# A transformer step on one core: the later modulation moved from VectorE to GpSimd, the first modulation in four column tiles

## The chip, the cores and the metric

The kernel runs on one core of a Trainium2 chip. The core has five engines that run their own instruction streams and wait for each other by semaphores: TensorE (PE), VectorE (DVE), ScalarE (ACT), GpSimd (POOL) and SyncE (SP, here the queue that issues the transfers). The metric is the device time of one execution in microseconds. Before the change it is 2648.65 us, the median of 3 runs (2647.0 to 2650.12).

## The reference

One inference step of one layer for two request groups, a prompt of 2048 tokens and a sample of 64 tokens, with 1024 channels. Cut to what matters here:

```python
def adaln(c, w, b):
    m = jax.nn.silu(c) @ w + b
    return jnp.split(m, 3, axis=-1)          # shift, scale, gate: 1024 columns each

shift, scale, gate = adaln(c, mod_mix_w[l], mod_mix_b[l])   # "modulation" of the mixers
h = modulate(x, norm_mix_g[l], shift, scale)
q, k, v, rx, rg, ga, gb = jnp.split(h @ w_in[l], SPLIT_POINTS, axis=-1)
# mixer A: banded attention over q, k, v;  mixer B: conv4 + gated linear recurrence over rx, GeLU gate rg
merged = sigmoid(ga) * (attn @ w_branch[l, :512]) + sigmoid(gb) * (rnn @ w_branch[l, 512:])
x = x + gate * (merged @ w_out[l])
shift, scale, gate = adaln(c, mod_ffn_w[l], mod_ffn_b[l])   # modulation of the feed-forward part
h = modulate(x, norm_ffn_g[l], shift, scale)
val, gt = jnp.split(causal_dwconv(h @ ffn_up_w[l], ...), 2, axis=-1)
x = x + gate * ((val * gelu(gt)) @ ffn_down_w[l])
```

A modulation is a product of two rows (`silu(c)` of prompt and sample, 1024 long) with a 1024 x 3072 matrix. Shift and scale of the mixers are needed at once (the "first modulation", 2048 columns). The mixers' gate and all three parts of the feed-forward part (4096 columns, the "later modulation") are needed only after the attention.

## The kernel before

**Stages.** First modulation on TensorE (0 to 41 us of the profiled span); normalised and modulated input and the value product (to 143); 16 projection rounds (143 to 784); attention (to about 1030); merge, output product, feed-forward up (to 2213) and down. Large products use a seven-product scheme (Strassen's, with the parts of each operand split in two f16 terms, three passes each).

**A projection round** `r` (0 to 15) makes two column blocks of the input product in 21 products (7 combinations `c` times 3 column thirds `q`), each 12 matmuls of 128 x 352. Round `r` is of kind `r % 4`: 0 recurrence input, 1 and 3 gates, 2 and 3 q and k. In each round ACT copies products out of PSUM (`copy`, `c21`) and makes the high halves of the next round's weights (`proj_hi`), DVE adds blocks (`p_block`), makes weight sums (`proj_sums`) and low halves (`proj_lo`). The recurrence of mixer B is threaded through rounds `4j` to `4j+2` in six chunks `s`: `tap` (ACT), `conv` (3 dependent DVE instructions), `chunk_hi` (ACT), `chunk_lo` (DVE), `gate_products` (6 matmuls, PE line 3085, at fixed places between the 21 products), `gates` (ACT), `recur1`, `recur2`, `rnn_product`, `rnn_lo` (DVE), `root`, `rnn_hi` (ACT). PE runs in program order, so it stands when the gate products of a chunk wait for that chunk's `chunk_lo` (line 2299), or when a bank has not been read yet. In ACT's order the last half of a gate row (`gate_rows_v`, line 1463, which waits for DVE's last block of the round) stands ahead of `c21` (line 1450), and `c21` frees the banks of the next round's first product.

**The later modulation ("ring").** It is computed as rows: `silu(c)` is broadcast to all partitions (`crow`, 2 x 1024), and 32 weight tiles (128 x 1024) come in 64 half tiles of 128 x 512 (and 4 half rows of `c` before them) through two buffers `dmw`. `ring_load(k)` on SP waits until step `k - 2` has been used (semaphore `dm_used`), `ring_step(k)` on DVE multiplies and sums a half tile twice (lines 2362 and 2364), once for the prompt and once for the sample. The table `RING_AT` sets in which rounds, and at which of seven places in a round, how many steps stand: 12 in round 3, 14 each in 7 and 11, 6 each in 4, 8 and 12, 10 in 15. `gate_columns` in the merge stage reads the sums.

**What sets the order.** Every engine's order is written out by hand. SP's queue is in order as well: in each round it issues the next round's weights (`round_tiles`), the recurrent gate weights (`gw`), the stores of finished gate rows (`gate_row`), recurrent outputs (`recurrent_store`) and q and k rows (`head_row`), then the ring's loads of that round. After round 15 come the loads of the first attention group (`queries_and_keys`, line 827 and 830; `values_and_bias`, line 836 for the bias band), which may start when products 1 and 2 of round 15 are done. DVE's `mask(0)` (line 2467) needs the band. DVE's `p_block` of a round of kind 2 needs the gate rows of the round before stored (it writes over them).

**The first modulation.** `modulation(g)`, g in the order 0, 2, 1, 3, makes 512 columns: 8 float32 matmuls with the 2 columns of `silu(c)` as stationary operand, accumulated in PSUM partitions 0 and 1; `mod_row` (ACT) copies the row out, and 4 transposes of a 2 x 128 piece turn it to columns, of which DVE makes coefficients.

GpSimd does nothing in the rounds; it modulates half of the input at 42 to 127 us, scales probabilities in the attention, and makes weight and activation sums in the feed-forward part.

## Time and profile before

| | |
|---|---|
| time, median of 3 | 2648.65 us |
| profiled execution, time | 2646.2 us |
| its span | 2644.4 us |
| PE busy | 2577.5 us, 97% |
| DVE busy | 1777.0 us, 67% |
| ACT busy | 1357.8 us, 51% |
| POOL busy | 556.5 us, 21% |
| granted clock, mean | 0.995 |

The span is what the trace covers; the profiled execution's time is 1.8 us longer. Start times in the rows are microseconds from the span's start. An instruction's duration includes a tail in which the next may already run, so starts that follow each other are closer than durations (a DVE instruction of 0.53 us repeats every 0.44 to 0.45 us). The mean duration of a matmul is longer than its place in the stream for the same reason: 72 matmuls of a round take 10.9 us. Matmul records can be missing.

### The profile page before, as it was taken

The numbers are of one execution on the slowest core, as the hardware profiler recorded it, in microseconds if no ns is written. First come the engines' busy times: TensorE is split into PE (matmuls) and PEld (weight loads), VectorE is DVE, ScalarE is ACT, GpSimd is POOL, SyncE is SP. The second block draws the span as 40 slices with busy tenths as digits, with TensorE's granted clock in tenths as the row PEclk, the third lists the DMA queues.
The fourth block names the chain that finished last, engine by engine and source line by source line (L and its number), as shares of the span: only waits on it lengthen the run. The fifth ranks groups of instructions, "written<-read, shape, count | busy, mean of one in ns | idle before, by whom it ended". The sixth has DMA issues, their size and how long they took to land.

```text
span 2644.4 us, 49826 instructions
## 1 busy us (share of the span) xinstructions
PE 2577.5 (97%) x18148; PEld 1676.1 (63%) x18148; DVE 1777.0 (67%) x3411; ACT 1357.8 (51%) x2631; POOL 556.5 (21%) x645
## 2 busy tenths in 40 slices
PE   7999999999989999999999999999999999999998
PEld 2456666665656665559996666666666666666665
DVE  5967677666756665566777798888888874242433
ACT  4967374563747774124556556555655553121211
POOL 2600000000007773000000354334333321101000
PEclk9999999999999999999999999999999999999999
DMA  8621523334255542556552355545454439566662
GB/s 290 198 98 63 208 81 113 102 108 136 79 144 145 108 161 84 184 180 156 136 145 71 122 193 173 187 162 177 167 187 167 157 112 362 206 235 242 228 248 99
DMA packets 243602, 424.07 MB, mean 160 GB/s; under 512 B 58392, under 2 KB 163352, under 8 KB 235240
## 3 DMA queue, kind: packets, MB, share of 16 engines
q1 hardware_dynamic: 234584, 413.08, 47.2%
q10 hardware_dynamic: 8848, 8.74, 1.0%
q8 instruction: 104, 1.70, 0.3%
q14 instruction: 66, 0.54, 0.1%
HBM read 284.47 MB, written 139.92 MB: 160 GB/s over the span
## 4 chain that ended last, share of the span: by engine, by line
PE 67%; issue 3%; ACT 2%; DVE 2%; POOL 1%; DMA 0%; SPq 0%; DVEq 0%; ACTq 0%; POOLq 0%
PE ps L3044 38%; PE ps L3299 16%; PE ps L3153 6%; PE ps L3143 2%; PE ps L3125 2%; PE ps L3112 1%; ACT arena L1641 1%; DMA arena<-in_w_down 0%; ACT arena L1652 0%; POOL arena L1212 0%; ACT arena L1739 0%; DVE arena L2641 0%; DVE arena L2716 0%; DVE arena L2720 0%; PE ps L3190 0%
## 5 line engine op out<-in xcount | busy, mean ns | idle before, releaser
L3044 PE MATMUL ps<-arena 128*128 128x352 f16 (+1 forms) x11880 | 1614.2, 297 | 12.1 <-ACT arena L1450 8.1
L3044 PEld LDWEIGHTS ps<-arena 128*128 128x128 f16 x11880 | 1100.6, 97 | 520.9 <-issue 9.7
L3299 PE MATMUL ps<-arena 128*128 128x352 f16 x2772 | 414.8, 310 | 0.0
L3299 PEld LDWEIGHTS ps<-arena 128*128 128x128 f16 x2772 | 264.7, 96 | 150.2 <-issue 1.0
L1212 POOL TENSOR_TENSOR arena<-arena 128x640 f32<-128x640 f32 (+5 forms) x136 | 150.0, 1121 | 723.1 <-DVE arena L2496 721.7
L1231 POOL TENSOR_TENSOR arena<-arena 128x128 f32<-128x128 f32 x44 | 31.0, 705 | 748.8 <-DMA arena<-in_w_down 748.6
L3153 PE MATMUL ps<-arena 128*128 128x424 f16 (+1 forms) x960 | 171.5, 341 | 0.0
L1801 ACT ACTIVATE arena<-ps 128x352 f32<-128x352 f32 x264 | 116.3, 461 | 92.7 <-PE ps L3044 92.5
L2848 DVE TENSOR_TENSOR arena<-ps,arena 128x352 f32<-128x352 f32 x12 | 6.3, 525 | 206.9 <-PE ps L3299 176.7
L1432 ACT ACTIVATE arena<-ps 128x352 f32<-128x352 f32 x192 | 80.7, 464 | 122.1 <-PE ps L3044 121.9
L3153 PEld LDWEIGHTS ps<-arena 128*128 128x128 f16 x960 | 92.5, 96 | 78.6
L1241 POOL TENSOR_TENSOR arena<-arena 128x176 f32<-128x176 f32 (+1 forms) x57 | 53.0, 931 | 399.1 <-DMA arena<-ffn_hidden 399.0
L2648 DVE SCALAR_TENSOR_TENSOR arena<-arena 128x512 f16<-128x512 f32 x154 | 105.3, 716 | 44.1 <-ACT arena L1763 44.1
L2716 DVE SCALAR_TENSOR_TENSOR arena<-arena 128x2114 f32<-128x2114 f32 x44 | 109.9, 2498 | 27.0 <-ACT arena L1838 26.9
L1641 ACT ACTIVATE arena<-arena 128x640 f32<-128x640 f32 (+5 forms) x136 | 103.3, 760 | 45.9 <-DVE arena L2480 45.5
L1994 ACT ACTIVATE arena<-ps 128x352 f32<-128x352 f32 x12 | 5.6, 464 | 206.3 <-PE ps L3299 206.3
L1844 ACT ACTIVATE arena<-arena 128x1057 f32<-128x1057 f32 x44 | 45.4, 1078 | 125.5 <-DVE arena L2720 125.5
L2720 DVE SCALAR_TENSOR_TENSOR arena<-arena 128x2114 f32<-128x2114 f32 x44 | 109.0, 2476 | 0.3
L1838 ACT ACTIVATE arena<-arena 128x2114 f32<-128x2114 f32 x44 | 94.7, 2151 | 26.2 <-DVE arena L2703 25.7
L2480 DVE CUSTOM_DVE_ANT_0 arena<-ps,arena 128x640 f32<-128x640 f32 (+5 forms) x136 | 95.9, 737 | 10.5 <-issue 9.9
L3013 PE MATMUL ps<-arena 128*128 128x512 f16 (+1 forms) x408 | 91.6, 382 | 7.3 <-DVE arena L2130 5.4
L3125 PE MATMUL ps<-arena 128*128 128x128 f32 (+1 forms) x600 | 89.9, 282 | 4.7 <-POOL arena L1212 2.9
(237 smaller groups left out, 3303.0 us busy)
## 6 DMA issues: line engine op xcount, KB each, us to landing
hidden_combinations<-arena SPq DMA_DIRECT2D x48, 616.0 KB, 3.2
arena<-hidden_combinations SPq DMA_DIRECT2D x24, 1232.0 KB, 7.9
arena<-in_w_up SPq DMA_DIRECT2D x44, 512.0 KB, 5.1
down_combinations<-arena SPq DMA_DIRECT2D x44, 448.0 KB, 2.8
ffn_hidden<-arena SPq DMA_DIRECT2D x44, 440.0 KB, 3.1
arena<-down_combinations SPq DMA_DIRECT2D x10, 1792.0 KB, 7.7
arena<-down_combinations SPq DMA_DIRECT2D x20, 896.0 KB, 6.3
arena<-ffn_hidden SPq DMA_DIRECT2D x50, 352.0 KB, 3.9
```

The source lines that it names most:

```text
L1212: pool.tensor_tensor(own, own, inv[0:x.rows, x.tile % 2, x.h:x.h + 1].to_broadcast([x.rows, x.w]), ALU.mult).then_inc(p_scaled, 1)
L1641: act.activation(pr[b][0:x.rows, x.h, 0:x.w], pr[b][0:x.rows, x.h, 0:x.w], ACT.Exp, scale=-1.0, bias=least[0:x.rows, x.h:x.h + 1], accum_o ...
L1801: act.activation(fcp[(0, 1, 2, 0)[i]][q], ps[:, bank_of((0, 2, 3, 4)[i], q), 0:CF], ACT.Copy, scale=CSF)\
L1838: act.activation(out, u[:, 0:LF], ACT.Identity, scale=w0, bias=fb).then_inc(f_tap, 1)
L2480: dve.tensor_tensor_reduce(pr[x.tile % 2][0:rows, h, 0:w], src, bias[x.b][0:rows, h, x.b0:x.b0 + w], 1.0, 3.0e38, ALU.add, ALU.min, least[ ...
L2648: dve.scalar_tensor_tensor(fsp[:, c, :, 1, :], src.rearrange("p (k m) -> p k m", k=4), -WSF if c == 6 else WSF, fsp[:, c, :, 0, :], ALU.mu ...
L2716: dve.scalar_tensor_tensor(out, u[:, 1:1 + LF], tap(1), out, ALU.mult, ALU.add).then_inc(f_conv, 1)
L2720: dve.scalar_tensor_tensor(out, u[:, 2:2 + LF], tap(2), out, ALU.mult, ALU.add).then_inc(f_conv, 1)
L3044: mm = pe.matmul(out, wt[:, k, wp, :], act_t[:, k, hp], start=(first and k == 0 and n == 0), stop=(last and k == K - 1 and n == 2), skip_g ...
L3125: mm = pe.transpose(ps[0:k, bank, c0:c0 + x.rows], pr[x.tile % 2][0:x.rows, x.h, c * P:c * P + k], ident[0:x.rows, 0:x.rows])
L3153: mm = pe.matmul(out, wt[:, wp, k, :], mixT[:, k, hp, t:t + w], start=(k == k0 and m == 0), stop=(k == k1 - 1 and m == 2))
L3299: mm = pe.matmul(ps[:, down_bank(n, k), 0:CF].rearrange("p (w t) -> p w t", w=2), dwt(i)[:, wi, wp, :], dact[i][:, :, bi, hp, :], start=(i ...
```

## The change

The later modulation leaves DVE. The weight tiles are now taken by halves of the input columns: first columns 0 to 511 of `c` and of all 32 tiles (34 steps: 2 half rows of `c`, 32 half tiles), then columns 512 to 1023. `crow` is therefore only 2 x 512 and is loaded and put through tanh twice (rounds 0 and 8). DVE keeps four instructions (`ring_row`, two at the end of round 0 and two at the end of round 8). Each half tile is done on GpSimd in eleven instructions: two products of 128 x 512 and nine halving sums of both together (2 x 256, 2 x 128, ... 2 x 1), each waiting for the one before. SP's loads are spread by `RING_LOTS`: 5 in most rounds from 1 to 14, none in round 15, and in rounds of kind 1 and 2 they stand between the recurrent stores. ACT's wait for `dm_used` goes, as its scratch row is no longer used by the ring. The first modulation's 8 matmuls of a group use a stationary operand of 32 columns (2 filled, 30 zero), and matmul `k` writes PSUM partitions `32 * (k % 4)` onward; the four partial rows are added by the matmul that turns them to columns, whose moving operand `pick` has ones at the four places.

```diff
-        NRING = 4 + 64
-        RING_AT = {3: (2, 2, 2, 2, 2, 0, 2), 4: (2, 2, 2), 7: (2,) * 7, 8: (2, 2, 2), 11: (2,) * 7, 12: (2, 2, 2),
-                   15: (2, 2, 2, 2, 2)}
+        HALF_RING = 2 + 32
+        NRING = 2 * HALF_RING
+        RING_LOTS = (0, 5, 5, 5, 5, 5, 5, 4, 2, 6, 5, 5, 6, 5, 5, 0)
+        CROW_ROUND = 8
...
             def ring_load(k):
-                cols = slice(512 * (k % 2), 512 * (k % 2) + 512)
+                half, step = k // HALF_RING, k % HALF_RING
+                cols = slice(512 * half, 512 * half + 512)
+                if step == 0:
+                    keep_above_zero(sp, dm_used, k)
+                    for s in range(2):
+                        sp.dma_start(crowv[:, s, :], a["c"][s:s + 1, cols].to_broadcast([P, 512])).then_inc(crow_loaded, 16)
                 keep_above_zero(sp, dm_used, k - 1)
...
-                if i == 1:
-                    for s in range(3):
-                        recurrent_store(j, s)
-                if i == 2:
-                    for s in range(3, NS):
-                        recurrent_store(j, s)
+                if i in (1, 2):
+                    recurrent_store(j, 3 * i - 3)
+                    recurrent_store(j, 3 * i - 2)
+                    ring_loads(r, 0, 3)
+                    recurrent_store(j, 3 * i - 1)
+                    ring_loads(r, 3, RING_LOTS[r])
...
+            def ring_tile(half, n):
+                m, k = 32 * half + n, HALF_RING * half + 2 + n
+                w = dmw[k % 2]
+                pool.wait_ge(dmw_loaded[k % 2], 64 + 16 * (k // 2))
+                pool.wait_ge(dm_used, k)
+                keep_above_zero(pool, ring_folded, 9 * m)
+                pool.tensor_tensor(dprod[:, 0], w, crowv[:, 0, :], ALU.mult)
+                pool.tensor_tensor(dprod[:, 1], w, crowv[:, 1, :], ALU.mult).then_inc(dm_used, 1)
+                pool.wait_ge(dm_used, k + 1)
+                size = 256
+                for step in range(9):
+                    keep_above_zero(pool, ring_folded, 9 * m + step)
+                    out = dprod[:, :, 0:size] if size > 1 else dpart[:, 2 * n:2 * n + 2, half:half + 1]
+                    pool.tensor_tensor(out, dprod[:, :, 0:size], dprod[:, :, size:2 * size], ALU.add)\
+                        .then_inc(ring_folded, 1)
+                    size //= 2
...
-                if j and s == 0:
-                    act.wait_ge(dm_used, ring_before(4 * j + 1))
...
-                mm = pe.matmul(ps[0:2, 4 + g, :], csv[:, k, :], mw[:, 4 * g:4 * g + 4, k, :],
-                               start=(k == 0), stop=(k == KT - 1))
+                own = slice(32 * (k % 4), 32 * (k % 4) + 32)
+                mm = pe.matmul(ps[own, 4 + g, :], csw[:, k, :], mw[:, 4 * g:4 * g + 4, k, :],
+                               start=(k < 4), stop=(k >= 4), skip_group_check=True)
```

**DVE, second half of round 7, before.** L2267 is a `p_block` of sums, L2264 the last `p_block`, L2200 `proj_lo`, L2362 and L2364 the two passes of a ring step with their accumulator reads; the piece is the part from `proj_lo` 3 to the last `p_block`.

```order
L2200 SCALAR_TENSOR_TENSOR arena<-arena 128x4x128
L2362 ISA arena<-arena 128x512
L2362 ISA arena 128x1
L2364 ISA arena<-arena 128x512
L2364 ISA arena 128x1
L2362 ISA arena<-arena 128x512
L2362 ISA arena 128x1
L2364 ISA arena<-arena 128x512
L2364 ISA arena 128x1
L2264 SCALAR_TENSOR_TENSOR arena<-ps,arena 128x352 x2
L2264 SCALAR_TENSOR_TENSOR arena<-ps,arena 128x320
```

The same place in the changed kernel (L2234 is `proj_lo`, L2298 the last `p_block`, L2295 the first of round 8):

```order
L2301 TENSOR_TENSOR arena<-arena 128x320
L2301 TENSOR_TENSOR arena<-arena 128x32
L2234 SCALAR_TENSOR_TENSOR arena<-arena 128x4x128
L2298 SCALAR_TENSOR_TENSOR arena<-ps,arena 128x352 x2
L2298 SCALAR_TENSOR_TENSOR arena<-ps,arena 128x320
L2298 SCALAR_TENSOR_TENSOR arena<-ps,arena 128x32
L2234 SCALAR_TENSOR_TENSOR arena<-arena 128x4x128 x2
L2295 SCALAR_TENSOR_TENSOR arena<-ps,arena 128x352 x2
```

No ring pass stands between the weights' low half and the last block of the round.

**SP, from the q and k rows of round 15 to the bias band, before.** L758 to L764 store q, k and the new keys, L783 is the ring, L827 and L830 load queries and keys of the first attention group, L836 the band.

```order
L763 DMA out_k_prompt<-arena 128x512
L764 DMA out_k_sample<-arena 128x64
L758 DMA keys<-arena 256x1x2048
L759 DMA keys<-arena 256x1x64
L783 DMA arena<-in_w_mod_rest 128x512 x8
L827 DMA arena<-queries 64x2112 x2
L830 DMA arena<-keys 64x2x2048
```

In the changed kernel (L765, L766, L760 and L761 are the same stores, L836 and L839 the loads of queries and keys):

```order
L765 DMA out_k_prompt<-arena 128x512
L766 DMA out_k_sample<-arena 128x64
L760 DMA keys<-arena 256x1x2048
L761 DMA keys<-arena 256x1x64
L836 DMA arena<-queries 64x2112 x2
L839 DMA arena<-keys 64x2x2048
```

The ring's last eight loads no longer stand ahead of the attention's loads. In rounds 13 and 14 they now stand among the stores (L728 loads the round's weights, L772 stores recurrent outputs, L790 is the ring, L754 and L755 store gate rows):

```order
L772 DMA recurrent_outputs<-arena 256x1x353
L790 DMA arena<-in_w_mod_rest 128x512 x2
L728 DMA arena<-in_w_proj 128x1024 x2
L754 DMA gates<-arena 128x2048
L755 DMA gates<-arena 128x64
```

So the store of the gate rows, which a `p_block` of the next round waits for, is queued behind ring loads that GpSimd paces.

## Rows read from the trace of the kernel before

**Rows 1.** Waits of PE, 150 to 800 us: released by, us, times, longest

```profile
PE ps L3044 <- ACT arena L1450: 8.1, 5, 4.6
PE ps L3085 <- issue: 6.1, 4, 1.9
```

**Rows 2.** Timeline of PE in the rounds: start us, us, instructions, [idle before]

```profile
322.80 1.06 PE L3085 MATMUL ps<-arena 128*128 128x353 f16 x6 [1.94 <-issue]
462.34 21.64 PE L3044 MATMUL ps<-arena 128*128 128x352 f16 x144 [2.96 <-ACT arena L1450]
...
624.61 23.32 PE L3044 MATMUL ps<-arena 128*128 128x352 f16 x144 [4.61 <-ACT arena L1450]
```

**Rows 3.** Timeline of ACT at the end of round 11

```profile
622.06 1.91 ACT L1463 ACTIVATE arena<-arena 128x2048 f32<-128x2048 f32 x1 [10.48 <-DVE arena L2264]
```

**Rows 4.** Groups by form on DVE, 582.3 to 624.6 us (round 11)

```profile
L2362 DVE CUSTOM_DVE_ANT_0 arena<-arena 128x512 f32<-128x512 f32 x14 | 9.7, 691 | 7.5 <-issue 5.6 <-DMA arena<-in_w_mod_rest 1.1
```

**Rows 5.** Timelines at the rounds' end: SP, then DVE, then PE

```profile
754.98 16.29 SPq L783 DMA_DIRECT2D arena<-in_w_mod_rest  x8
...
779.19 0.45 SPq L836 DMA_DIRECT2D arena<-band  x1
...
791.86 0.17 DVE L2467 MEMSET arena<- 64x128 f32 x1 [12.66 <-DMA arena<-band]
...
790.48 0.59 PE L3112 MATMUL ps<-arena 128*128 128x128 f16 x4 [6.53 <-DMA arena<-keys]
```

**Rows 6.** Timelines at the start: ACT, then DVE

```profile
39.59 0.59 ACT L1361 ACTIVATE arena<-ps 2x512 f32<-2x512 f32 x1 [1.85 <-PE ps L2968]
...
40.68 0.50 DVE L2089 TENSOR_TENSOR arena<-ps,arena 128x4 f32<-128x4 f32 x4 [1.08 <-PE ps L2975]
```

**Rows 7.** Groups by form on POOL, whole span: busy us, mean ns

```profile
L1212 POOL TENSOR_TENSOR arena<-arena 128x512 f32<-128x512 f32 x8 | 8.2, 1040 | 3.2 <-DVE arena L2496 3.2
L1212 POOL TENSOR_TENSOR arena<-arena 128x128 f32<-128x128 f32 x8 | 3.2, 400 | 674.6 <-DVE arena L2496 674.6
```

**Rows 8.** Timeline of POOL, 1448 to 1450 us: the second waits for the first

```profile
1448.32 0.46 POOL L1231 TENSOR_TENSOR arena<-arena 128x128 f32<-128x128 f32 x1 [7.53 <-DMA arena<-in_w_down]
1448.86 0.45 POOL L1233 TENSOR_TENSOR arena<-arena 128x128 f32<-128x128 f32 x1
```

**Rows 9.** POOL and DVE at once: timelines, and line 2506 alone

```profile
1007.21 2.46 POOL L1212 TENSOR_TENSOR arena<-arena 128x640 f32<-128x640 f32 x2 [0.61 <-DVE arena L2496]
1008.45 2.30 DVE L2506 SCALAR_TENSOR_TENSOR arena<-arena 128x1024 f16<-128x1024 f32 x1
...
L2506 DVE SCALAR_TENSOR_TENSOR arena<-arena x8: 1216/1226/2297, 1008.5 to 1167.7; 128x1024 f16<-128x1024 f32 x8
```

**Rows 10.** Busy us by stretch: PE, PEld, DVE, ACT, POOL; rounds 5 and 6

```profile
342.80:383.10 40.30, 40.25 (x270) 26.12 (x271) 28.93 (x57) 32.11 (x54) 0.00 (x0) 1.00 0.12 41
383.10:421.60 38.50, 38.50 (x260) 24.90 (x258) 25.61 (x52) 24.48 (x46) 0.00 (x0) 1.00 0.29 99
```

**Rows 11.** Timelines of DVE and PE in rounds 5 and 6

```profile
357.56 0.52 DVE L2299 SCALAR_TENSOR_TENSOR arena<-arena 128x353 f16<-128x353 f32 x1
358.96 1.06 PE L3085 MATMUL ps<-arena 128*128 128x353 f16 x6
379.79 0.53 DVE L2299 SCALAR_TENSOR_TENSOR arena<-arena 128x353 f16<-128x353 f32 x1
382.24 1.06 PE L3085 MATMUL ps<-arena 128*128 128x353 f16 x6
395.61 1.45 DVE L2261 SCALAR_TENSOR_TENSOR arena<-ps,arena 128x352 f32<-128x352 f32 x4 [0.36 <-DMA gates<-arena]
396.98 0.51 DVE L2299 SCALAR_TENSOR_TENSOR arena<-arena 128x350 f16<-128x350 f32 x1
399.25 1.05 PE L3085 MATMUL ps<-arena 128*128 128x350 f16 x6
```

**Rows 12.** Timeline of SP in round 6: weights of round 7, then the gate rows

```profile
386.51 0.81 SPq L726 DMA_DIRECT2D arena<-in_w_proj  x2
```

More of the change, by code:

```diff
@@ L168, in build @@
         sm, inv = (at_(o, 4).rearrange("p (b h) -> p b h", b=2) for o in (47812, 47816))
-        crow = at_(51816, 2 * D)
+        crow = at_(51816, 2 * 512)
         crowv = crow.rearrange("p (s d) -> p s d", s=2)
-        dmw = [at_(53864 + 512 * i, 512) for i in range(2)]
-        djunk = at_(36628, 512)
+        dmw = [at_(52840 + 512 * i, 512) for i in range(2)]
+        dprod = at_(53864, 2 * 512).rearrange("p (s d) -> p s d", s=2)
         dpart = at_(54888, 2 * 64).rearrange("p (n w) -> p n w", w=2)
@@ L814, in _ @@
                     head_row(j, 1)
-                for k in range(ring_before(r) + 2, min(ring_before(r + 1) + 2, NRING)):
-                    ring_load(k)
+                if i in (0, 3):
+                    ring_loads(r, 0, RING_LOTS[r])
                 if r == 3:
@@ L1185, in _ @@
                 modulate0(e)
+            def ring_tile(half, n):
[14 more added lines that the diff above has]
+                    size //= 2
+            for half in range(2):
+                for n in range(32):
+                    ring_tile(half, n)
             def cached_halves(j):
@@ L2349, in rnn_lo, with ring_row @@
                     .then_inc(x_lo, 1)
[L2351 to L2374 removed]
+            def ring_row(half):
+                dve.wait_ge(crow_sig, half + 1)
+                for step in range(2):
+                    k = HALF_RING * half + step
+                    dve.wait_ge(dmw_loaded[k % 2], 64 + 16 * (k // 2))
+                    part = crowv[:, step, :]
+                    dve.scalar_tensor_tensor(part, part, 1.0, dmw[k % 2], ALU.add, ALU.mult).then_inc(dm_used, 1)
             for r in range(NR):
@@ L2379, in _ @@
                 proj_lo(r, 6)
-                ring(r, 0)
                 if i == 1:
@@ L2392, in _ @@
                     p_block(r, 0, q)
-                if i == 3:
-                    ring(r, 1)
                 if i == 1:
@@ L2422, in _ @@
                             chunk_lo(j, 3)
-                ring(r, 3)
                 if i == 0:
@@ L2436, in _ @@
                     p_block(r, 2, q)
-                ring(r, 4)
                 if i == 0:
@@ L2447, in _ @@
                     proj_lo(r + 1, 4)
-                ring(r, 5)
                 if i == 1:
@@ L2452, in _ @@
                     p_block(r, 1, q)
-                ring(r, 6)
+                if r in (0, CROW_ROUND):
+                    ring_row(r // CROW_ROUND)
                 if i == 0:
```

59 lines of the change are left out of this document (22 added, 37 removed).

## The prediction

> **What bounds the kernel now.** I began with the page's busy shares: PE is busy 97% of the span, the others 21 to 67%, so time can come or go only where PE stands. PE's list of waits, cut to the projection rounds, shows where [rows 1]: 8.1 us in five waits for ACT's line 1450 and 6.1 us in four waits of the gate products. The timeline of PE places them [rows 2]: 4.61 us at the start of round 12, 2.96 us at that of round 8, 1.94 us before the first gate products of round 4; the other six, 0.15 to 1.64 us each, lie in rounds 4, 5, 8, 9, 12 and 13. They stand in or right behind the rounds in which DVE has ring steps. At the end of round 11 ACT waits 10.48 us for DVE's last block before it can make the gate row that is ahead of line 1450 in its order [rows 3]; DVE ran 14 passes of 691 ns there for the prompt and as many for the sample, and stood some 5 us more for half tiles to come [rows 4]. So the ring, and not PE alone, ends these waits. The same 144 matmuls of products 0 to 3 take 21.64 us behind the short stall and 23.32 us behind the long one [rows 2], another 1.7 us.
>
> At the rounds' end the timelines of SP, DVE and PE belong together [rows 5]: SP issues eight ring loads from 755.0 to 771.3 us, each after DVE has used a buffer, and only then the queries and keys; the band is issued at 779.19 and DVE gets it at 791.86, while PE waits from 783.95 on. At the start, ACT waits 1.85 us for the last group of the first modulation and DVE 1.08 us for its columns [rows 6].
>
> **The change, part by part.**
>
> *Rounds, what goes.* All nine waits [rows 1] have a ring step, or a load queued behind one, in their cause: 8.1 + 6.1 = 14.2 us, with the 1.7 us of the long stall 15.9 us. What is late next is the question of the port below.
>
> *End of the rounds.* Round 15 has no ring, so queries and keys can be issued once product 1 of round 15 is done (PE is through round 15 at 790.48 - 6.53 = 783.95; its 252 matmuls take 252 x 0.150 = 37.9 us, so it begins at 746, and 72 matmuls later it is 757), and the band 8 us later (779.19 - 771.3), at 765. It landed 12.7 us after issue, so at about 778, before PE is free. PE's first scores then follow the last block at about 784.5 instead of 790.48, and DVE has its mask ready: between 6 us (PE's wait alone) and 7.5 us (from 784.4 to 791.86). I take 7.0.
>
> *First modulation.* TensorE's part of the last group is shorter if the four column tiles run beside each other, and as long as before if they do not; no row shows it. What waits for it is ACT with 1.85 us and DVE with 1.08 us in front of the coefficients, and the earlier groups wait for their weights' transfers. So it gives 0 to 1.9 us; I take DVE's 1.1, as DVE's own work is next in line. The added zero fill and `pick` lie before the first weights have landed: nothing.
>
> *GpSimd's half tile, alone.* Two widths of one line give 640 ns for 384 elements more, so 1.667 ns an element and 187 ns a piece [rows 7]. A half tile has 3 pieces of 512 elements (two products and the first sum), and 256, 128 ... 2: 2046 elements, 3.41 us, and 11 x 0.187 = 2.06 us. A piece that waits for the one before starts 0.08 us after its end (1448.86 against 1448.32 + 0.46) [rows 8]; ten of these are 0.8 us. Sum 6.3 us, 64 half tiles 401 us. The trace has no piece of under 128 elements, so the small ones may be off by the whole 187 ns.
>
> *The port.* What happens when DVE reads two operands from SBUF while GpSimd does is shown at 1007 us [rows 9]: GpSimd's two pieces took 2.46 us, as long as alone, and DVE's line 2506, issued as the second began, took 2.30 us where the seven others take about 1.22. It stood for the whole of GpSimd's piece. The Trainium skill says the same in "SBUF — State Buffer", section "Who interferes with whom": a DVE instruction with two SBUF inputs contends with a GpSimd instruction that reads SBUF, the first to start has the port and the other fully blocks. "Perfetto Trace Analysis", section "Optimizing Scalar/DVE Operations", adds that moving work between the two might therefore not help; by that rule alone this change should bring nothing, and the price of rival 2 is what it would be here.
>
> In round 5 DVE is busy 28.93 of 40.3 us [rows 10], all but some 3 us of it with two SBUF inputs. Five half tiles hold the port 5 x 3.41 = 17.1 us. About 26 + 17 = 43 us of port in a round of 40.3: in rounds of kind 1 it is oversubscribed, and GpSimd falls behind there. In round 6 it is 24 + 17 = 41 of 38.5 us at most; kinds 0 and 3 have room. If both engines take turns all the time, each of GpSimd's 11 pieces waits for one DVE instruction of about 0.5 us: 3.41 + 5.5 = 8.9 us a half tile. Between 6.3 and 8.9 I take 8.0 us. DVE in turn is held 3.41 / 11 = 0.31 us for each instruction.
>
> *Who waits for the delayed DVE.* The low half of chunk 2 (line 2299) ends 0.9 us before its gate products in round 5, that of chunk 4 1.9 us before, that of chunk 5 in round 6 1.8 us before [rows 11]. Before chunk 2 six such instructions depend on each other through ACT: 6 x 0.31 = 1.9 us, stall 1.0, of which I count 0.8. Before chunk 4 there are some sixteen, less what two idle stretches take up: 3.9 us, stall 2.0. Chunk 5: 0.5. Chunk 0 (rounds 4 and 12; no GpSimd work yet in round 0 and nothing to load in 8) has five and nearly no slack: 1.4. With chunk 4 alone in the first group at full price the four groups are 2.5 + 4.7 + 3.3 + 4.7 = 15.2 us. At the two ends: 0 if DVE's pauses take it all up, and twice that, 30 us, if every wait for ACT moves with DVE.
>
> *What the SP queue adds.* SP's loads wait for GpSimd's products now. The last load before the weights of round 14 needs 27 half tiles multiplied in the second half of the ring. That half starts at about 506 us (its row steps stand at the end of round 8, which begins at 462.34 and holds 264 matmuls, 39.7 us, and short waits; then a load), and SP issues the weights and gate rows of that round some 3.4 us after its start (386.51 against 383.1 in round 6) [rows 12], at 711 (round 14 ends 37.9 us ahead of round 15's start, with 6 gate matmuls, so it begins at 707.6). With 8.0 us a half tile, whose products are done 0.3 of the way through it, it is 506 + 26.3 x 8.0 = 716; DVE's `p_block` waits for a gate row's store already (0.36 us), with 1.8 us to spare behind it [rows 11]. The overrun of 3 us lies in the same stretch as the 4.7 us above, which move all of it later; nothing is added.
>
> *What costs nothing.* ACT's wait for `dm_used` and the shorter `crow`: the traffic is the same 16 MB, spread wider. The second tanh of `crow` on ACT in round 8 (half of the 1.91 us that 2048 columns take [rows 3]) lies in ACT's idle time.
>
> *Sum.* 15.9 + 7.0 + 1.1 - 15.2 = 8.8 us less: 2646.2 - 8.8 = 2637.4 for the profiled execution. The median of the runs is 2.4 us above that execution, so 2640.
>
> **The rivals.**
>
> 1. *DVE's pauses take up all the delays.* For it: DVE idles 11 us in round 5, mostly waiting for ACT. Against it: those pauses are links of the same chain. Cost 0 to 5: 24 us less, 2625.
>
> 2. *The port gives all of it back.* The stalls before the gate products reach 24 us, since the blocking adds up along chains through ACT: 2648.65, no change. Any cost of 19 to 29 us ends here.
>
> 3. *GpSimd cannot keep pace, slower.* The place is SP's queue: each ring load waits for GpSimd, and weights, gate-row stores and recurrent stores wait behind it. GpSimd's first half tile comes behind the second recurrent store of round 1, 15 us into it (357.56 - 342.8 in round 5) [rows 10, 11] and a load, about 201 us. At 8.9 us a half tile the last load of round 5 comes at 201 + 22.3 x 8.9 = 399.5 us against 386.5, the one of round 13 at 506 + 26.3 x 8.9 = 740 against 711. Less 1.8 us of slack each, 11 + 27 = 38 us: 2648.65 - 24 + 38 = 2663. It decides from about 8.5 us a half tile, where 2 + 17 us of overrun with the rest of the chunk stalls eat up the 24. For it: the sums of port time for rounds 5 and 6 exceed the round. Against it: rounds of kind 3 leave the port half free, and every stall of PE gives GpSimd time.
>
> 4. *The column tiles do not run beside each other.* Then 1.1 us less is gained: 2641, inside the forecast's own range.
>
> **How the numbers follow.** The forecast has 0.40 (with rival 4), rival 1 0.15, rival 2 0.17, rival 3 0.28. About 0.2%, 5.3 us, is what a measurement here can tell from no change. The forecast's own range is 2631 to 2645; a seventh of it lies within the 5.3 us, so faster is 0.35 + 0.15 = 0.50, the same 0.05 + 0.17 = 0.22, slower 0.28. The range that should hold 8 in 10 goes from the full saving, 2622, to just above the price of rival 3, 2664.
>
> **What would show it.** Of the changed kernel: no wait of PE at the start of rounds 8 and 12 over 1 us, and none of 1.3 us before the second gate products of rounds 8 and 12; PE's first scores within 2 us of its last projection product, and the band landed before. On POOL eleven pieces per half tile, spaced 8 us in mean from 205 to 760 us, the 512-wide ones 1.04 us where DVE is idle. On DVE `conv` of 0.53 to 0.58 us stretched to 0.8 and over. Small new waits of PE, 1 to 2 us, before the gate products of chunks 2 and 4. If these reach 4 us and more, or if the projection weights are issued later than 8 us into a round, rivals 2 and 3 hold. I am wrong altogether if half tiles take 6.5 us in busy rounds, which would mean that the port is seldom fought over.

## The result, and the profile after

The changed kernel takes 2709.53 us, the median of 4 runs (2707.01 to 2710.24); the kernel before took 2649.39 beside it (4 runs, 2647.0 to 2652.43). The ratio is 1.0224, 95% interval 1.0211 to 1.0237: 60 us slower, where 2640 was forecast and 2664 was the range's upper end.

The busy shares on the changed kernel's page (us, share of the span of 2705.2 us), and PE's list of waits from 150 to 852 us (waited for, us, times, longest):

```profile
PE 2585.1 (96%) x18164; PEld 1683.8 (62%) x18164; DVE 1836.7 (68%) x3157; ACT 1355.8 (50%) x2632; POOL 1082.3 (40%) x1349
```

```profile
PE ps L3097 <- issue: 54.4, 8, 14.8
PE ps L3056 <- ACT arena L1481: 6.9, 4, 2.9
PE ps L3097 <- DVE arena L2333: 5.0, 4, 1.6
```

Line 3097 holds the gate products (3085 before) and line 2333 is `chunk_lo`. Where PE had waited 14.2 us [rows 1], it now waits 66.3 us, nearly all before the gate products. PE's timeline has the places:

```profile
227.27 1.93 PE L3097 MATMUL ps<-arena 128*128 128x353 f16 x6 [5.66 <-issue]
...
344.72 1.93 PE L3097 MATMUL ps<-arena 128*128 128x353 f16 x6 [11.00 <-issue]
...
384.01 1.06 PE L3097 MATMUL ps<-arena 128*128 128x353 f16 x6 [2.75 <-issue]
412.75 1.93 PE L3097 MATMUL ps<-arena 128*128 128x353 f16 x6 [5.30 <-issue]
433.67 1.05 PE L3097 MATMUL ps<-arena 128*128 128x350 f16 x6 [1.64 <-DVE arena L2333]
458.68 59.23 PE L3056 MATMUL ps<-arena 128*128 128x352 f16 x396 [2.48 <-ACT arena L1481]
...
740.13 1.93 PE L3097 MATMUL ps<-arena 128*128 128x353 f16 x6 [14.76 <-issue]
741.85 12.33 PE L3056 MATMUL ps<-arena 128*128 128x352 f16 x72
...
852.63 0.40 PE L3124 MATMUL ps<-arena 128*128 128x128 f16 x4 [0.62 <-ACT arena L1484]
```

Two patterns are mixed. One comes again in the groups of a kind 1 and a kind 2 round: in rounds 5 and 6 (384 to 434 us) 2.75, 5.30 and 1.64 us before chunks 2, 4 and 5, and 2.48 at the start of the next kind 3 round. Before chunk 4 it stands in all four groups (4.51 to 6.20 us), the others are smaller in some or missing. The other is single and long: 11.00 us before chunk 0 of round 4, 14.76 before chunk 2 of round 13 (and 4.22 before chunk 0 of round 12).
The wait of 14.76 us is read on SP's timeline, with ACT and DVE behind it. Line 790 is a load of the ring, 728 the next round's weights, 772 a recurrent store, 1565 `rnn_hi`, 2382 `rnn_lo`:

```profile
683.81 46.65 SPq L790 DMA_DIRECT2D arena<-in_w_mod_rest  x6
730.50 0.91 SPq L728 DMA_DIRECT2D arena<-in_w_proj  x2
731.45 8.15 SPq L772 DMA_DIRECT2D recurrent_outputs<-arena  x2
```

```profile
737.29 0.50 ACT L1565 ACTIVATE arena<-arena 128x353 f16<-128x353 f32 x1 [16.92 <-DMA recurrent_outputs<-arena]
```

```profile
737.82 1.23 DVE L2382 SCALAR_TENSOR_TENSOR arena<-arena 128x353 f16<-128x353 f32 x1 [11.64 <-ACT arena L1565]
738.98 1.05 DVE L2333 SCALAR_TENSOR_TENSOR arena<-arena 128x353 f16<-128x353 f32 x1
```

Six ring loads, each waiting for GpSimd to give a buffer free, hold the queue for 46.65 us, so the recurrent store of chunk 0 leaves at 731.45; its staging buffer is the one that `rnn_hi` of chunk 1 fills; `rnn_lo`, the low half of chunk 2 and PE's products stand behind. The wait of 11.00 us in round 4 ends with another transfer, the gate weights of the recurrence, which SP issued at 327.44 us, right behind five ring loads that held it for 34.11 us, the transfer of the bias band (320.05) and round 5's weights:

```profile
340.29 0.42 ACT L1534 ACTIVATE arena<-arena 128x256 f16<-128x256 f32 x1 [11.44 <-DMA arena<-in_w_rgate]
```

In SP's list of waits (180 to 852 us) the ring loads read:

```profile
SPq L790 <- POOL arena L1203: 290.8, 43, 14.0
```

The short waits are read from the groups on DVE, after (180 to 852 us; busy us, mean ns | idle before):

```profile
L2234 DVE SCALAR_TENSOR_TENSOR arena<-arena 128x512 f16<-128x512 f32 x100 | 98.0, 1008 | 31.2 <-ACT arena L1442 31.2
L2323 DVE SCALAR_TENSOR_TENSOR arena<-arena 128x353 f32<-128x353 f32 x54 | 47.0, 871 | 2.5 <-ACT arena L1529 1.1
L2357 DVE TENSOR_TENSOR_SCAN arena<-arena 128x353 f32<-128x353 f32 x19 | 25.2, 1329 | 0.7
```

The same three before were 686, 584 and 944 ns (180 to 784 us):

```profile
L2200 DVE SCALAR_TENSOR_TENSOR arena<-arena 128x512 f16<-128x512 f32 x100 | 66.1, 686 | 18.8 <-ACT arena L1411 18.8
L2289 DVE SCALAR_TENSOR_TENSOR arena<-arena 128x353 f32<-128x353 f32 x54 | 31.6, 584 | 2.9 <-ACT arena L1498 1.6
L2323 DVE TENSOR_TENSOR_SCAN arena<-arena 128x353 f32<-128x353 f32 x19 | 17.9, 944 | 0.7
```

GpSimd's own timeline, where DVE idles (727.6 us), shows a half tile alone: the next begins 7.23 us after it, against a median spacing of 9.37 us.

```profile
727.62 1.26 POOL L1202 TENSOR_TENSOR arena<-arena 128x512 f32<-128x512 f32 x1 [0.17 <-POOL arena L1209]
...
734.85 1.26 POOL L1202 TENSOR_TENSOR arena<-arena 128x512 f32<-128x512 f32 x1 [0.17 <-POOL arena L1209]
```

So two theories stood: theory 1, the queue (GpSimd's pace, through SP's order, holds up other transfers); theory 2, the port (GpSimd's reads stretch DVE, so that the chunks are late whatever SP does).

### The profile page after: what moved, and what is told of

Read it like the earlier page. It is cut to its first block, busy times and chain, and to the rows that moved or that the text cites. A ratio compares the mean times of both kernels' runs of the same rounds, so it can differ in the third digit from the quotient of the medians.

```text
span 2705.2 us, 50375 instructions
## 1 busy us (share of the span) xinstructions
PE 2585.1 (96%) x18164; PEld 1683.8 (62%) x18164; DVE 1836.7 (68%) x3157; ACT 1355.8 (50%) x2632; POOL 1082.3 (40%) x1349
## 4 chain that ended last, share of the span: by engine, by line
PE 62%; POOL 5%; DVE 5%; issue 4%; ACT 3%; DMA 1%; SPq 0%; DVEq 0%; ACTq 0%; POOLq 0%
PE ps L3056 34%; PE ps L3311 15%; PE ps L3165 6%; POOL arena L1209 3%; PE ps L3155 2%; PE ps L3137 2%; PE ps L3124 1%; POOL arena L1203 1%; ACT arena L1670 1%; DMA arena<-in_w_down 1%; DVE arena L2726 0%; DVE arena L2730 0%; ACT arena L1681 0%; DVE arena L2323 0%; ACT arena L1768 0%
## 5 line engine op out<-in xcount | busy, mean ns | idle before, releaser
L1209 POOL TENSOR_TENSOR arena<-arena 128x512 f32<-128x512 f32 (+8 forms) x576 | 343.3, 596 | 45.1
L1202 POOL TENSOR_TENSOR arena<-arena 128x512 f32<-128x512 f32 x64 | 86.5, 1351 | 132.0 <-DMA arena<-in_w_mod_rest 122.2
L2658 DVE SCALAR_TENSOR_TENSOR arena<-arena 128x512 f16<-128x512 f32 x154 | 104.4, 710 | 45.7 <-ACT arena L1792 45.7
L2234 DVE SCALAR_TENSOR_TENSOR arena<-arena 128x512 f16<-128x512 f32 x112 | 105.8, 974 | 31.6 <-ACT arena L1442 31.4
```

The costliest lines, as they stand in the source:

```text
L1209: pool.tensor_tensor(out, dprod[:, :, 0:size], dprod[:, :, size:2 * size], ALU.add)\
L2234: dve.scalar_tensor_tensor(fsp0[:, c, :, 1, :], src.rearrange("p (k m) -> p k m", k=4), -WSF if c == 6 else WSF, fsp0[:, c, :, 0, :], ALU. ...
L2658: dve.scalar_tensor_tensor(fsp[:, c, :, 1, :], src.rearrange("p (k m) -> p k m", k=4), -WSF if c == 6 else WSF, fsp[:, c, :, 0, :], ALU.mu ...
```

## The experiments

All are edits of the changed kernel, but for the one on the first modulation.

### The two theories apart

No ring loads behind the first two half tiles; GpSimd multiplies and sums these 64 times.

```diff
             def ring_loads(r, n0, n1):
-                for k in range(ring_before(r) + 2 + n0, min(ring_before(r) + 2 + n1, NRING)):
-                    ring_load(k)
+                for k in range(ring_before(r) + 2 + n0, ring_before(r) + 2 + n1):
+                    if k < 4:
+                        ring_load(k)
```

> The changed kernel with the loads of the later modulation left out behind the first two half tiles; GpSimd does the same eleven instructions 64 times on the two tiles that it has, so its port use stays and nothing of it stands in SP's queue (the second pair of half rows of c goes too, so the later modulation's values are not those of the reference). Theory 1 (SP's queue: loads paced by GpSimd stand ahead of weights, gate weights and recurrent stores): the stalls of 5 to 15 us before the gate products go, what is left is the port's 10 to 20 us; 2635 to 2650 us, at least 55 us below the changed kernel's 2709.5. Theory 2 (port: DVE's stretched instructions make the low half of the chunks late by themselves): still above 2690. Half tiles spaced 9.0 to 9.6 us in mean as before, or less, since PE's stalls no longer give GpSimd quiet time.

Measured: 2684.73 us, ratio to before 1.014 (1.0125 to 1.0155). It fell by 25 us, not by 55, and stays 36.5 us above the kernel before; neither theory had this. PE's timeline keeps the repeating pattern and has lost the single long waits:

```profile
371.36 1.06 PE L3102 MATMUL ps<-arena 128*128 128x353 f16 x6 [2.78 <-issue]
...
400.30 1.93 PE L3102 MATMUL ps<-arena 128*128 128x353 f16 x6 [5.50 <-issue]
421.43 1.05 PE L3102 MATMUL ps<-arena 128*128 128x350 f16 x6 [2.12 <-DVE arena L2338]
446.45 13.73 PE L3061 MATMUL ps<-arena 128*128 128x352 f16 x91 [2.49 <-ACT arena L1486]
```

The other way round: fills that read nothing, with the loads still waiting for them.

```diff
-                pool.tensor_tensor(dprod[:, 0], w, crowv[:, 0, :], ALU.mult)
-                pool.tensor_tensor(dprod[:, 1], w, crowv[:, 1, :], ALU.mult).then_inc(dm_used, 1)
...
+                        pool.memset(dprod[:, :, 0:480], 0.001).then_inc(ring_folded, 1)   # nine times
```

> The changed kernel with GpSimd's arithmetic on a half tile replaced by nine fills of 128 x 960 and one small one, which read nothing from SBUF, at the same pace (about 9.3 us a half tile, the buffer given free after the third) and with the same loads waiting for it in SP's queue; the later modulation is not computed. Theory 1 (queue and pace): 2695 to 2715 us, with the same long waits of the gate products for loads that SP issues late. Theory 2 (port): DVE's conv is back at 0.58 us and the time is 2625 to 2650. Should the fills take 0.85 us each rather than 0.93, the pace is 8.6 us and theory 1 gives 2670 to 2690.

Measured: 2677.44 us, ratio 1.0109 (1.0094 to 1.0124), at 8.86 us a half tile, in the range that was expected of the queue at the shorter pace. The long waits are there; the repeating ones of 2.8 and 5.5 us before chunks 2 and 4 are not:

```profile
336.59 1.93 PE L3100 MATMUL ps<-arena 128*128 128x353 f16 x6 [15.01 <-issue]
...
714.51 1.93 PE L3100 MATMUL ps<-arena 128*128 128x353 f16 x6 [12.44 <-issue]
```

Before chunk 5 PE waits 2.88, 4.72 and 5.34 us in rounds 6, 10 and 14, more than without loads, and DVE's timeline has the cause in round 6: its block waits for the gate rows' store, which stands behind ring loads on SP.

```profile
413.48 1.45 DVE L2298 SCALAR_TENSOR_TENSOR arena<-ps,arena 128x352 f32<-128x352 f32 x4 [5.07 <-DMA gates<-arena]
415.46 1.91 PE L3100 MATMUL ps<-arena 128*128 128x350 f16 x6 [2.88 <-DVE arena L2336]
```

DVE's `conv` is back at 586 ns, and DVE's busy time over the span is 1698.0 us; it was 1843.8 without loads. Both theories are true: the long waits are the queue's, those before chunk 4 the port's. A wait before chunk 5 can be of either; in the changed kernel DVE's list of waits has none for the gate rows' store.

### The queue: from which pace

The same fills, shorter: 704 and 832 elements in place of 960.

> The kernel e2_fill_tiles with fills of 128 x 704, so about 7 us a half tile (the price that GpSimd has alone) instead of 9; the later modulation is not computed. The prediction put the point from which SP's queue decides at about 8.5 us a half tile. If the queue stalls come from the pace: all three stalls of 4 to 15 us go, 2632 to 2645 us. If they come from the order alone (loads between the recurrent stores, whatever the pace): they stay near the 2677 us of e2_fill_tiles.

> The kernel e2_fill_tiles with fills of 128 x 832, about 7.9 us a half tile; the later modulation is not computed. At 8.86 us a half tile the queue cost 2677.4 us, at 6.94 nothing (2621.3). The prediction took 8.0 us and added nothing for the queue. By its sum for the second half (a load of round 13 at 506 + 26.3 x 7.9 = 714 against 711, and 1.8 us of slack): at most 2 us a place, 2621 to 2626 us. If the queue decides earlier than the prediction put it (at the rounds with five or six loads, each of which must be done within 38 to 40 us of its round: 5 x 7.9 = 39.5): 2630 to 2650.

Measured: 2621.29 us (ratio 0.9896, 0.9881 to 0.9912) at 6.94 us a half tile, without any wait of PE in the rounds, 11 us under what was expected of the pace; and 2641.24 us (0.9972, 0.9961 to 0.9983) with 832 elements. So, measured from the first of them, 6.9, 7.9 and 8.9 us a half tile cost 0, 20 and 56 us by the queue alone. The middle one falls under the second alternative: the queue begins to cost between 6.9 and 7.9 us. Two of its waits carry it:

```profile
327.01 1.93 PE L3100 MATMUL ps<-arena 128*128 128x353 f16 x6 [6.78 <-issue]
...
683.39 1.93 PE L3100 MATMUL ps<-arena 128*128 128x353 f16 x6 [6.40 <-issue]
```

### The port: by piece, by time, by place

GpSimd stops each half tile after the sum of 2 x 64, the fifth piece (from the kernel without loads).

```diff
-                for step in range(9):
+                for step in range(3):
```

> The kernel e1_no_loads with GpSimd's half tile cut to its two products and the first three sums (512, 256, 128 and 64 wide): 5 pieces and 1920 of 2046 elements, so the later modulation is not computed. Measured by DVE's busy time over the whole span, which was 1843.8 us in e1_no_loads and 1698.0 with GpSimd's fills: 146 us of stretching, 2.28 us a half tile. If the port is lost by the piece (each of GpSimd's pieces stops one DVE instruction for about 0.21 us): 5/11 of it, DVE busy 1760 to 1770 and time 2655 to 2668. If it is lost by the time that GpSimd's operands take: nearly all of it stays, DVE busy 1815 to 1845; time then 2665 to 2682, as the half tiles follow each other more densely and end sooner.

Measured: 2721.89 us, ratio 1.0275 (1.0259 to 1.0291), DVE busy 1859.7 us, half tiles 6.37 us apart in median. The stretching did not shrink with the pieces, so it goes by the time of the wide ones; but the time is 40 us above the 2665 to 2682 that were expected of this. With less work on GpSimd the kernel got slower by 37 us. Over the 1698.0 us with fills, DVE was held 2.5 us by each half tile, where it had been 2.3, but these now come every 6.37 us and not every 9.29: the wide pieces follow each other without the small ones. That the small pieces were the time in which DVE got on is the reading of this; no run spaces the wide pieces in another way. PE's timeline in round 1:

```profile
234.61 1.93 PE L3104 MATMUL ps<-arena 128*128 128x353 f16 x6 [11.01 <-issue]
```

Then by place: 24 half tiles from the start of rounds 3, 7 and 11, or from the start of rounds 5, 9 and 13.

```diff
+            for lot in range(3):
+                pool.wait_ge(p_filled, p_done(4 * lot + 2, 6, 2))      # e12_chain_rounds: 4 * lot + 4
+                for n in range(8):
+                    ring_tile(0, 8 * lot + n)
```

> The kernel e1_no_loads with 24 of the 64 half tiles on GpSimd, eight from the start of rounds 3, 7 and 11 (kind 3, then kind 0), none in rounds of kinds 1 and 2; the rest of the later modulation is left out. The port alone cost 63.4 us for 64 half tiles (2684.7 against 2621.3 with fills of 6.94 us), 1.0 us each. If each half tile costs its share wherever it stands: 24 us, 2643 to 2648. If the cost arises where DVE's work is a chain that the gate products wait for and is dense (kinds 1 and 2): under 8 us, 2622 to 2629.

> The kernel e10_quiet_rounds with the same 24 half tiles of GpSimd put into the other rounds, eight each from the start of rounds 5, 9 and 13 (kind 1, then kind 2); the rest of the later modulation is left out. e10_quiet_rounds, with rounds of kinds 3 and 0, took 2620.2 us, nothing for the port. In e1_no_loads each group of a kind 1 and a kind 2 round had waits of 2.8, 5.5 and 2.1 us before the gate products and 2.5 us at the start of the next round. If the port costs in these rounds alone: three times 10 to 13 us and 1 us of clock each, 2652 to 2662 us. If e10_quiet_rounds was cheap only because 24 half tiles are few: 2620 to 2630.

Measured: 2620.19 us (0.9892, 0.9877 to 0.9907) in rounds of kinds 3 and 0, 2652.98 us (1.0016, 1.0006 to 1.0025) in kinds 1 and 2: the same work, 33 us apart, the first 2 us under its range and the second in it. The first has no wait of PE in the rounds at all; the second has in each of its three groups the waits before chunks 4 and 5 that the kernel without loads had, and 0.9 us before chunk 2. The first group:

```profile
354.63 1.06 PE L3103 MATMUL ps<-arena 128*128 128x353 f16 x6 [0.92 <-issue]
383.27 1.93 PE L3103 MATMUL ps<-arena 128*128 128x353 f16 x6 [5.20 <-issue]
404.41 1.05 PE L3103 MATMUL ps<-arena 128*128 128x350 f16 x6 [1.85 <-DVE arena L2339]
```

The 24 half tiles stretch DVE in the quiet rounds too (DVE busy 1730.1 us against 1695.6 with the short fills), where PE waits for none of it. They do so by 1.4 us each, and in kinds 1 and 2 by 2.9 (1764.3 us): the place counts twice, as DVE has less to be held there and nothing that PE waits for. How much of the 33 us is owed to each is not separated. Windows without stretching (kernel with short fills; us, then busy us of PE, PEld, DVE, ACT and POOL) show the room, in rounds 3, 4 and 5 (kinds 3, 0 and 1):

```profile
262.00:302.00 40.00, 40.00 (x270) 25.87 (x269) 14.43 (x25) 16.73 (x31) 36.20 (x58) 1.00 0.43 151
302.00:337.00 35.00, 35.00 (x236) 22.61 (x235) 19.27 (x39) 17.84 (x36) 24.30 (x39) 1.00 0.45 168
337.00:377.00 40.00, 40.00 (x271) 25.85 (x269) 28.47 (x56) 31.88 (x53) 35.12 (x58) 1.00 0.27 80
```

### The first modulation alone

The kernel before with the four column tiles and nothing else.

> The kernel before with the first modulation in four column tiles and nothing else. The changed kernel resumed its value stage 0.7 us earlier, so 0.5 to 1.0 us less than before, 2648.0 to 2648.9; if the column tiles cost something later, above 2649.5. Either way within 0.1% of the kernel before.

Measured: 2649.23 us, ratio 1.0006 (0.9997 to 1.0015). No gain that can be measured; its value stage resumes at 57.72 us, 0.75 before the 58.47 of the kernel before.

### Halves and spread, on DVE

GpSimd's half tile goes; DVE does it with two fused passes as before the change, by halves, in an order of its own.

```diff
+            def ring_step(k):
+                half, n = k // HALF_RING, k % HALF_RING - 2
+                w = dmw[k % 2]
+                dve.wait_ge(dmw_loaded[k % 2], 64 + 16 * (k // 2))
+                dve.wait_ge(dm_used, k)
+                for s in range(2):
+                    ins = dve.tensor_tensor_reduce(dprod[:, s], w, crowv[:, s, :], 1.0, 0.0, ALU.mult, ALU.add,
+                                                   dpart[:, 2 * n + s, half:half + 1])
+                ins.then_inc(dm_used, 1)
+        RING_AT = {1: (0, 0, 0, 0, 0, 0, 0), 2: (0, 0, 0, 0, 0, 1, 1), 3: (1, 2, 1, 2, 1, 2, 2), ..., 14: (0, 0, 0, 0, 1, 2, 3), 15: (2, 1)}
```

> The changed kernel's halves, first modulation and a round 15 nearly free of steps, but the half tiles are multiplied and summed on DVE by its two fused passes, 1 step in rounds of kind 1, 2 to 6 in kinds 0 and 2, 11 in rounds 3, 7 and 11, 3 at the start of round 15. If spreading and the early loads of the attention were the good part and GpSimd the bad one: no port conflict and a step of 1.5 us that never paces SP for long, so the 6 us at the end of the rounds and about 8 of the 14 us in the rounds stay gained: 2632 to 2640 us, faster than both. If the spreading itself (steps in rounds whose chain is tight) was at fault: above 2650.

Measured: 2641.17 us, ratio 0.997 (0.9959 to 0.9982), 1 us above the range that was expected if GpSimd was the bad part. Four waits were left: 2.95, 4.38, 4.09 us at round starts, 2.47 us before chunk 0 of round 4. On DVE's timeline of round 14 a step stood 3.24 us for its half tile just ahead of the last block. So the next kernel moves steps from in front of the last blocks to behind them, in rounds 3, 7, 10, 11 and 14. In round 4 it puts three at the very start, ahead of the first chunk's low half (three of the changed entries):

```diff
-  4: (0, 0, 1, 1, 1, 2, 0), ... 11: (1, 2, 1, 2, 1, 2, 2), ... 14: (0, 0, 0, 0, 1, 2, 3),
+  4: (1, 2, 0, 1, 1, 1, 0), ... 11: (1, 1, 1, 1, 1, 0, 6), ... 14: (0, 0, 0, 0, 1, 0, 5),     # the last place is behind the last block
```

> The kernel e3_on_dve with its steps placed otherwise: in rounds of kind 3, 2 and 1 none stands in the last stretch before DVE's last block of the round, and 1 to 6 stand behind it, where DVE idled 5 to 10 us into the next round. e3_on_dve had four waits of PE at round starts (2.95, 4.38, 4.09 and 0.20 us, each behind a last block that was late by ring steps) and 2.5 us before the first gate products of round 4. If late blocks behind steps that wait for their half tiles are the cause: these 11.6 us go, 2628 to 2633 us. If DVE's total work in these rounds is the bound: the stalls move to the gate products of rounds 4, 8 and 12, and it stays at 2638 to 2643.

Measured: 2636.53 us, ratio 0.9956 (0.9943 to 0.997). The waits at round starts are gone, as the first alternative had it, but one of 12.72 us came before chunk 0 of round 4, so neither number was met. It came with the steps moved forward in round 4: one that needed a new load stood for it, with `chunk_lo` behind.

```profile
327.39 0.69 DVE L2378 CUSTOM_DVE_ANT_0 arena<-arena 128x512 f32<-128x512 f32 x1 [17.02 <-DMA arena<-in_w_mod_rest]
```

So three steps of round 4 go behind that chunk (and round 2 gets one more):

```diff
-  3: (1, 1, 1, 1, 1, 0, 4), 4: (1, 2, 0, 1, 1, 1, 0),
+  3: (1, 1, 1, 1, 1, 0, 4), 4: (0, 0, 0, 0, 2, 2, 1),
```

> The kernel e5_placed with three steps of round 4 moved from in front of the first chunk's low half to behind it (round 4 then has 5 steps, all in its second half, round 2 one more). In e5_placed one wait was left in the rounds, 12.72 us before the first gate products of round 4: DVE stood 17.0 us for a half tile that SP issued at 314.1 us, behind the transfer of the bias band, and with it stood the low half of the gate weights and of chunk 0. If that is all: this wait goes and nothing comes in its place, 2621 to 2626 us, as fast as the kernel without any later modulation on DVE (e7_fill_short, 2621.3). If the late half tile only moves the wait to the second gate products of round 4: 2628 to 2634.

Measured: 2631.68 us, ratio 0.9937 (0.9924 to 0.9951). The number is in the second alternative's range, but its mechanism is not what happened: the second gate products wait for nothing, and 6.50 us of the wait before the first are still there. On SP's timeline the gate weights of the recurrence (line 811) leave right behind the transfer of the bias band (line 828):

```profile
300.90 0.76 SPq L828 DMA_DIRECT2D band<-bias_rows  x1
301.73 6.49 SPq L729 DMA_DIRECT2D arena<-in_w_proj  x2
308.33 0.69 SPq L811 DMA_DIRECT2D arena<-in_w_rgate  x1
```

```diff
-                if r == 3:
+                if r == 0:
                     sp.wait_ge(bias_rows_stored, 16)
                     sp.dma_start(band_d.rearrange("q h n -> h q n"), ...)
```

One ring step also moves, from round 15 to round 12.

> The kernel e8_placed_again with the transfer that spreads the bias band issued in round 0 instead of round 3, and one ring step moved from round 15 to round 12. In e8_placed_again the one wait left in the rounds was 6.50 us before the first gate products of round 4: the recurrence's gate weights were issued at 308.3 us behind the band transfer (300.9), and the half tiles before. If the band transfer holds them up: that wait and the 0.8 + 1.9 us at the first scores go, 2621 to 2624 us, 1.0% below the kernel before. If it is SP's lateness alone (the ring loads of round 3 end at 300.5): 2 to 6 us of the wait stay, 2625 to 2629.

Measured: **2622.45 us, ratio 0.9896 (0.9879 to 0.9912)**, with the whole computation in it: 26 us faster than the kernel before and 87 us faster than the changed one. The ring loads of round 3 end no earlier than in the kernel before it (302.0 us against 300.9), but without the band in between the next transfers take 0.80 us to issue, not 6.49, and the gate weights land at most 7.4 us after issue, not 13.6. So it was the band, and not SP's lateness:

```profile
302.91 0.80 SPq L729 DMA_DIRECT2D arena<-in_w_proj  x2
303.83 0.37 SPq L811 DMA_DIRECT2D arena<-in_w_rgate  x1
```

The longest wait of PE that is left in the rounds (list of waits, 150 to 852 us):

```profile
PE ps L3100 <- DVE arena L2312: 0.6, 1, 0.6
```

It does all of the later modulation on DVE and is 1 to 2 us from the kernels that leave most or all of it out: 2622.45 against 2621.29 and 2620.19. The band's early transfer was not tried in the kernel before by itself; PE's waits there before the first two gate products of round 4, 1.94 and 1.64 us, are the ones that it could bear on.

## Why the prediction was wrong

**What bounds the kernel: right.** The waits that were to go were the ring's, and their sum with the end of the rounds, 24 us, was near: without ring steps on DVE and without a queue stall the time is 2621.3, 27 us below the kernel before. (The 2622 in its range is 24 us off the profiled execution; off the median it is 2624.7.)

**End of the rounds: right.** The wait before the first scores fell from 6.53 to 0.62 us, and that before the next ones, for DVE, from 1.58 to 0.42: 7.1 us together, where 7.0 was taken.

**First modulation: right in the trace, not to be seen in the time.** The column tiles do run side by side. The last group's 16 matmul records took 7.05 us before, the first row, and 2.85 after, the second, though at a granted clock of 0.66 and not 1.00 (two other groups of the changed kernel took 1.93 us at 1.00 and 3.64 at 0.50):

```profile
32.50 7.05 PE L2968 MATMUL ps<-arena 128*2 128x512 f32 x16
```

```profile
32.86 2.85 PE L2979 MATMUL ps<-arena 128*32 128x512 f32 x16
```

The value stage began 0.7 us earlier, as ACT and DVE stand behind; in time the change alone is within its interval of nothing.

**The half tile alone: too small.** The prediction had 6.3 us, the trace 7.23. The step that failed is the price of an element: 1.667 ns came from two rows whose second operand is a broadcast column [rows 7]. The 512-wide product of two full tiles takes 1.26 us, not 1.04. The rows of two full operands were on the table (0.46 us for 128 elements [rows 8], where the formula gives 0.40) and were used for the wait alone. The Trainium skill, "GPSIMD Engine Reference", section "Elementwise — side-by-side cycle accounting", gives about 2.6 cycles an element for a tensor-tensor operation, at 1.2 GHz 2.17 ns. By estimate the 2046 elements then take 4.4 us in place of 3.41, and with the prediction's own 2.06 and 0.8 us for starts and waits the half tile takes 7.3. The trace, 7.23, agrees with it and not with the prediction.

**Full turn-taking as 8.9, taken as 8.0: too small.** The half tiles came 9.37 us apart in median, and 9.29 in the kernel without loads.

**The SP queue: the step that failed most.** "The overrun of 3 us lies in the same stretch ...; nothing is added." At 7.9 us a half tile the queue alone costs 20 us, at 8.9 us 56. The sum looked at one load, the last one ahead of round 14's weights, and asked how late it was. What waits behind the loads is more than weights: the recurrent store of chunk 0, without which `rnn_hi` of the next chunk can't write (14.76 us), the gate weights of the recurrence behind the bias band in round 4 (11.00 us), and with the fills the store of the gate rows. Rival 3 named the queue and these stores and had round 13 among its places; its point, 8.5 us, was too high, its price, 38 us, too low, and it had nothing for round 4.

**The port's delay: right on average, wrong in the chain.** 0.31 us an instruction was foreseen and 0.29 (`conv`) to 0.39 (scan) measured over all. But the port alone cost 63 us (2684.7 against 2621.3), not 15.2. The prediction had small new waits of 1 to 2 us before chunks 2 and 4, and 4 us and more as the sign of rivals 2 and 3: this sign is there, in all four groups. In the kernel without loads the low half of chunk 4 is 7.4 us later than before (5.5 us of wait and the 1.9 of slack [rows 11]), where 3.9 was taken. The timeline of DVE between chunks 2 and 4 there shows why:

```profile
375.61 1.25 DVE L2349 TENSOR_TENSOR arena<-arena 128x353 f32<-128x353 f32 x1 [0.28 <-ACT arena L1559]
376.89 1.48 DVE L2351 SCALAR_TENSOR_TENSOR arena<-arena 128x353 f32<-128x353 f32 x1
378.29 2.37 DVE L2328 SCALAR_TENSOR_TENSOR arena<-arena 128x353 f32<-128x353 f32 x3
...
384.62 1.62 DVE L2358 TENSOR_TENSOR arena<-arena 128x353 f32<-128x353 f32 x1 [1.12 <-ACT arena L1564]
386.27 1.84 DVE L2362 TENSOR_TENSOR_SCAN arena<-arena 128x353 f32<-128x353 f32 x1
```

An instruction that comes after a pause, or waits for the one before it, finds GpSimd inside a wide piece and stands 0.7 to 1.1 us (1.25, 1.48 and 1.62 against 0.53); the mean is made low by others that lose nothing (the median of `conv` there is 0.59 us, as before, while the medians of lines 2349 and 2358 are 1.24 and 1.36). The chain consists of such instructions. Blocks that take one operand from PSUM (lines 2300 and 2303 there, 522 and 516 ns in mean; 523 and 521 with the fills) were not stretched at all. And the round was full: DVE busy 39.7 of 43.8 us in round 5, so there was nothing to catch up with. That the late chain also delays the last block (2.5 us each at the starts of rounds 3, 7, 11 and 15) had no term. The prediction's own check, "43 us of port in a round of 40.3", was the right reading, and was then spent on GpSimd's pace alone.

**The rule of the shared port.** The Trainium skill, "SBUF — State Buffer", section "Who interferes with whom", calls the shared port pair an exclusive lock, and says that a DVE instruction with two SBUF inputs contends with a GpSimd instruction that reads SBUF. The rows above agree (1.25 and 1.62 us against 0.53). The Trainium skill, "Perfetto Trace Analysis", section "Optimizing Scalar/DVE Operations", warns that such a move may not help. The prediction took this as no gain at all (rival 2, 2648.65); the port alone, measured, made 2684.7, worse than that, because the delays fall on the chain. Where they fall decides: in rounds with 14 us of DVE work in 40, or 19 in 35, such half tiles were free.

**Sum.** The parts, measured: 27 us gained (2648.4 to 2621.3), 63 lost by the port alone and 56 by the queue alone (at 8.86 us). Together they are not 119 but 88 (2709.5 - 2621.3). That waits of one kind give time to the other, as a PE that stands for the queue lets DVE catch up, would explain it; no run shows it by itself.

Left open: how much of the 11.00 us in round 4 is the band transfer's and how much SP's lateness. In the changed kernel the band was not moved by itself; at 6.94 us a half tile it stands in the same place of the queue and PE waits for nothing.

## What to carry to other kernels

Give the second engine work that shares the port only where the first one has room and no one waits for a chain on it, and take the delay of a chained instruction from the longest piece that it can meet, not from the mean. Before loads are tied to a slower engine, go through everything that stands behind them in the same in-order queue and ask what each one's consumer is, the small stores first. When a move to another engine disappoints, its gain may lie in the reordering alone: here halving, spreading, 1.5 us steps behind the last block of a round and the band's transfer in round 0 gave 26 of the 27 us without GpSimd.

## What was unexpected in the hardware

- Cutting GpSimd's half tile from eleven pieces to five (6.37 us apart, not 9.29) made the kernel 37 us slower. The six pieces that went were small, 0.3 to 0.5 us each in the changed kernel.
- A GpSimd product of two full 128 x 512 float32 tiles took 1.26 us alone, against 1.04 with a broadcast second operand [rows 7]; fills of 128 x 960 took 0.90 us and left DVE's instructions at their length.
- The bias band's transfer between two DRAM buffers, issued in 0.76 us, held back the load of the gate weights behind it, which landed 13.6 us after issue, and at most 7.4 with the band in round 0: with the band in front PE waited 6.5 us; with it in round 0 (and one ring step moved) nothing.
